# A table decides which picks' V rows VectorE sums: from a flat quarter to 0 to 12 of each 16

## The chip, the cores and the metric

The kernel runs as one program on one core of a Trainium2 chip. The metric is the device time of one execution in microseconds; the median of several runs counts.

## The reference

One inference step of a two-layer decoder in fp32, for 512 prompt tokens and 8 sample tokens, width 1024. Each layer is a recurrent mixer (layer 0: gated DeltaNet and Mamba-2 side by side; layer 1: gated linear attention) and then a PEER block, which picks for each token 8 x 16 = 128 of 16384 single-neuron experts:

```python
v1, i1 = lax.top_k(s1, PEER_TOPK)
v2, i2 = lax.top_k(s2, PEER_TOPK)
cand = (v1[..., :, None] + v2[..., None, :]).reshape(...)
top_s, top_j = lax.top_k(cand, PEER_TOPK)
expert = jnp.take_along_axis(cand_idx, top_j, axis=-1)
gate = jax.nn.softmax(top_s, axis=-1)
pre = jnp.einsum('thkd,td->thk', u_tab[expert], tb)
act = jax.nn.gelu(pre) * gate
return jnp.einsum('thk,thkd->td', act, v_tab[expert])
```

The tables are too large for on-chip memory, so each pick is a gather of one U row and one V row (8 KB together) for each of 128 tokens: 1 MB.

## The kernel before

**Units and picks.** Tokens are cut into tiles of 128 prompt tokens and one of 8 sample tokens. A unit is one layer and one tile; the ten units are the outer loop (layer 0: tiles 0, 1, sample, 2, 3, then layer 1 the same), and units 2 and 7 are those of the sample. A unit of prompt tokens has 128 picks, one of the sample 8, in all 1040 picks, numbered by g. In this text a stretch is 16 picks of one unit, from the dot product of its first pick to that of the next stretch.

**One pick.** GpSimd (POOL) issues the gather into one of 7 slots of `ring` (L456). VectorE (DVE) waits for it, multiplies the U half with the tokens and sums: the dot product (L1817). ScalarE (ACT) makes gelu of it (`act_v`), multiplies by the gate (`gated`) and, for most picks, scales the identity matrix by it into one of 4 slots of `diag`. TensorE (PE) then multiplies `diag` with the V half of the slot, two products 128x512 that add up in PSUM banks 0 and 1 over the unit. That counts `v_done`, and the slot is free for the gather of pick g + 7.

**Picks aside.** For picks marked in the table `ASIDE` no `diag` is made and PE does nothing. Instead VectorE multiplies the V half by the weight and adds it to `otok` (`add_v`, L1778; the first of a unit only multiplies, L1776), after the dot product of pick g + 2, and counts `side_done`, for which POOL waits then. At the end of a unit VectorE adds PSUM to `otok` (`join_out`, L1785), and PE transposes it back. `SUMMED` and `TURNED` count the picks of either kind up to g, and every engine takes its waits from them.

```python
ASIDE = [t != S and u < 8 and k % 4 == 2 for u, (_, t) in enumerate(UNITS) for k in range(COUNT[u])]
```

**The other work.** The mixers, the output and query projections and the rankings of later tiles (top 16, twice) are generators that yield a slot, the number of a pick; each engine runs all their work of slot g behind its work for pick g (`front.upto(g)`, `choose.upto(g)`), PE two picks ahead (`LEAD`). Weight products (`ps<-hT,wring`) take 6 matmuls of PE a slot, and SyncE loads their weights in blocks of 512 KB into 3 slots of `wring`. So the table of slots fixes which stretches stand beside products, convolutions, scans or rankings. Rankings run on VectorE (L1643 to L1678). Every engine works in order.

Of the kernel before, what the change touches and what calls it, by code (L numbers as in the profile page):

```python
# [36 lines left out]
S = 4  # L37
# [11 lines left out]
UNITS = [(L, t) for L in range(2) for t in (0, 1, S, 2, 3)]  # L49
COUNT = [NS_TOK if t == S else NPICK for _, t in UNITS]  # L50
FIRST = [sum(COUNT[:u]) for u in range(len(UNITS) + 1)]


ASIDE = [t != S and u < 8 and k % 4 == 2 for u, (_, t) in enumerate(UNITS) for k in range(COUNT[u])]
SUMMED = [sum(ASIDE[:g]) for g in range(len(ASIDE) + 1)]
TURNED = [g - n for g, n in enumerate(SUMMED)]
HAS_ASIDE = [any(ASIDE[FIRST[u]:FIRST[u + 1]]) for u in range(len(UNITS))]
HSLOT = (0, 1, 0, 1, 2)
# [51 lines left out]
def build_program(nc, io):  # L110
# [5 lines left out]
    with ExitStack() as ctx:  # L116
# [5 lines left out]
        def sem(name):  # L122
            if name not in sems:
                sems[name] = ctx.enter_context(nc.semaphore(name))
            return sems[name]
# [235 lines left out]
        def _(pool):  # L361
# [82 lines left out]
            for u, (L, t) in enumerate(UNITS):  # L444
# [4 lines left out]
                for k in range(COUNT[u]):  # L449
                    g = FIRST[u] + k  # L450
                    index = tail_pick[:, k:k + 1] if t == S else picked[:, HSLOT[t], k:k + 1]
                    if g >= RING and ASIDE[g - RING]:
                        pool.wait_ge(sem("side_done"), SUMMED[g - RING + 1])
# [15 lines left out]
        def _(pe):  # L469
# [396 lines left out]
            for u, (L, t) in enumerate(UNITS):  # L866
# [9 lines left out]
                for k in range(COUNT[u]):  # L876
                    g = FIRST[u] + k
                    if not ASIDE[g]:
                        pe.wait_ge(sem("weighed"), TURNED[g + 1])
# [22 lines left out]
        def _(act):  # L902
            def f(out, in_, func, **k):
                return act.activation(out, in_, func, **k)  # L904
# [213 lines left out]
            for u, (L, t) in enumerate(UNITS):  # L1118
                for k in range(COUNT[u]):
# [6 lines left out]
                    f(gated[:, s:s + 1], act_v[:, s:s + 1], ACT.Copy, scale=gate).then_inc(sem("gated"), 1)  # L1126
                    if not ASIDE[g]:
                        act.wait_ge(sem("gated"), g + 1)
# [20 lines left out]
        def _(dve):  # L1149
# [619 lines left out]
            def add_v(g):  # L1769
                u = [v for v in range(len(UNITS)) if FIRST[v] <= g][-1]  # L1770
                weight = gated[:, g % SMALL:g % SMALL + 1]
                dve.wait_ge(sem("gated"), g + 1)
                if SUMMED[g] == SUMMED[FIRST[u]]:
                    if u:
                        dve.wait_ge(sem("out_mm"), u)
                    last = tsc(otok[:, :], ring[:, g % RING, D:2 * D], weight, None, MUL)  # L1776
                else:
                    last = stt(otok[:, :], ring[:, g % RING, D:2 * D], weight, otok[:, :], MUL, ADD)  # L1778
                last.then_inc(sem("side_done"), 1)

            def join_out(u):
                dve.wait_ge(sem("v_done"), TURNED[FIRST[u + 1]])
                dve.wait_ge(sem("side_done"), SUMMED[FIRST[u + 1]])
                x = otok.rearrange("p (b i) -> p b i", b=2)
                tt(x, x, ps[:, 0:2, :], ADD).then_inc(sem("otok_ready"), 1)  # L1785

            def add_out(u):
                dve.wait_ge(sem("out_mm"), u + 1)
                t = UNITS[u][1]
                x = xT[:, :, TILE_AT[t]:TILE_AT[t] + ROWS[t]]  # L1790
                if t == S:
                    y = ps[:, 0, 0:KD * NS_TOK].rearrange("p (c b) -> p c b", c=KD)
                else:
                    y = ps[:, 0:2, :].rearrange("p b (c i) -> p (b c) i", c=4)
                tt(x, x, y, ADD).then_inc(sem("added"), 1)
# [4 lines left out]
            for u, (L, t) in enumerate(UNITS):  # L1800
                if t != S:
                    dve.wait_ge(sem("htok_ready"), u + 1)
                if t == S:
                    add_v(FIRST[u] - 2)
                    join_out(u - 1)
                for k in range(COUNT[u]):
                    g = FIRST[u] + k
                    if t == S:
                        dve.wait_ge(sem("spread"), L * NS_TOK + k + 1)
                        h = ps[:, 4 + 2 * (k % 2):6 + 2 * (k % 2), :]  # L1810
                    else:
                        h = htok[:, HSLOT[t], :]
                    dve.wait_ge(sem(f"uv_loaded{g % RING}"), 16 * (g // RING + 1))
                    x = ring[:, g % RING, 0:D]
                    if t == S:
                        x = x.rearrange("p (b i) -> p b i", b=2)
                    stt(x, x, 1.0, h, MUL, MUL, accum_out=pre[:, g % SMALL:g % SMALL + 1]).then_inc(sem("dotted"), 1)  # L1817
                    if g >= 2 and ASIDE[g - 2] and not (t == S and k == 0):
                        add_v(g - 2)
                    if k == 0 and u and t != S and HAS_ASIDE[u - 1]:  # L1820
                        join_out(u - 1)
                    if k == 1 and u:
                        add_out(u - 1)
                    front.upto(g)
                    choose.upto(g)
# [116 lines left out]
```

## Time and profile before

| | |
|---|---|
| median of 3 runs | 3783.91 us (3767.95 to 3787.49) |
| profiled execution | 3767.21 us, its span 3765.4 us |
| PE / DVE / ACT / POOL busy | 78% / 65% / 32% / 33% |
| HBM traffic over the span | 325 GB/s |
| dot products L1817 | 1024 + 16, 1226 ns each for 128x1024 |
| adds L1778 | 186, 1286 ns each |
| gathers L456 | 1024 in the largest group, 1151 ns of issue each |

Busy shares are averages over stretches with different limits, so the reading goes by stretch. In tables by stretch a line has the stretch in us from the span's start, its length, and then busy us with the number of instructions for PE, PEld (weight load of PE, which overlaps PE), DVE, ACT and POOL; then the granted clock of PE as a share of full speed, the mean busy share of the 16 DMA engines, and GB/s moved.

### The profile page before, as it was taken

Reading aid. Unit: us, or ns where it says so; the run is one execution under the profiler, and the core shown is the slowest. Engines: PE = TensorE matmul, PEld = TensorE weight load, DVE = VectorE, ACT = ScalarE, POOL = GpSimd, SP = SyncE. Lnnn points to the kernel's source line nnn. Section 1 sums busy time; section 2 is a strip of 40 time slices with the busy share of each in tenths; the row PEclk is TensorE's granted clock in tenths of the full one; section 3 lists DMA queues with packets and bytes.
Section 4 is the critical chain, followed back from the end, with each engine's and each line's share of the span. In section 5 each row is a group of like instructions: output and inputs, shape, how many; then the busy total and the mean of one; then the engine's idle time right before and its main releaser. Section 6 shows DMA issues by size and latency. Waiting matters only on the chain.

```text
span 3765.4 us, 31261 instructions
## 1 busy us (share of the span) xinstructions
PE 2942.9 (78%) x9704; PEld 1695.3 (45%) x9704; DVE 2448.8 (65%) x5019; ACT 1190.9 (32%) x3448; POOL 1245.4 (33%) x1094
## 2 busy tenths in 40 slices
PE   7667478788789769998976679887896678778776
PEld 6556345455556325655632237454563223222222
DVE  4333579688665778676569787557656958645444
ACT  1211133533233323343333332422333324334333
POOL 0000022355333423343345433334334434434332
PEclk9788788899789979989989889888899889999999
DMA  4102187899899979988999999879899879999996
GB/s 153 55 1 90 56 315 264 321 374 364 323 360 392 385 274 342 360 334 344 395 417 412 373 396 364 329 291 404 338 391 406 338 287 412 395 420 418 417 420 287
DMA packets 183658, 1225.39 MB, mean 325 GB/s; under 512 B 21185, under 2 KB 21585, under 8 KB 48194
## 3 DMA queue, kind: packets, MB, share of 16 engines
q0 software_dynamic: 153088, 1115.26, 74.7%
q1 hardware_dynamic: 30402, 108.12, 7.7%
q8 instruction: 77, 1.26, 0.1%
q14 instruction: 91, 0.75, 0.1%
HBM read 1211.46 MB, written 11.84 MB: 325 GB/s over the span
## 4 chain that ended last, share of the span: by engine, by line
PE 42%; DVE 25%; DMA 20%; ACT 4%; issue 3%; DVEq 2%; POOL 2%; SPq 0%; ACTq 0%; POOLq 0%
PE ps L471 42%; DMA ring<-in_uv,picked 19%; DVE ring L1817 7%; DVE otok L1778 2%; POOL ring L456 2%; ACT scratch L904 2%; DVE scratch L1645 1%; DVE scratch L1647 1%; DVE scratch L1651 1%; DVEq L1641 1%; DVE scratch L1643 1%; DVE scratch L1676 1%; DVE scratch L1671 1%; DVE ids L1678 1%; ACT diag L904 1%
## 5 line engine op out<-in xcount | busy, mean ns | idle before, releaser
L471 PE MATMUL ps<-ring,diag 128*128 128x512 f32 x3392 | 1782.2, 658 | 493.8 <-ACT diag L904 485.5
L456 POOL DMA_INDIRECT ring<-in_uv,picked x1024 | 1178.7, 1151 | 2100.7 <-PE ps L471 1413.7
L1817 DVE SCALAR_TENSOR_TENSOR ring<-ring,htok 128x1024 f32<-128x1024 f32 x1024 | 1246.1, 1226 | 653.1 <-DMA ring<-in_uv,picked 639.6
L471 PEld LDWEIGHTS ps<-ring,diag 128*128 128x128 f32 x3392 | 645.3, 204 | 1379.7 <-ACT diag L904 826.1
L471 PE MATMUL ps<-hT,wring 128*128 128x256 f32 (+1 forms) x3200 | 744.2, 388 | 62.2 <-DVE hT L1187 28.2
L904 ACT ACTIVATE act_v<-pre 128x1 f32<-128x1 f32 x1040 | 209.6, 202 | 1697.0 <-DVE ring L1817 1687.6
L471 PEld LDWEIGHTS ps<-hT,wring 128*128 128x128 f32 x3200 | 618.0, 194 | 232.0 <-issue 97.2
L904 ACT ACTIVATE diag<-masks,gated 128x128 f32<-128x128 f32 x832 | 334.1, 402 | 44.6 <-PE ps L471 17.4
L904 ACT ACTIVATE gated<-act_v,gates 128x1 f32<-128x1 f32 x1024 | 301.6, 295 | 33.3
L471 PE MATMUL ps<-scratch 128*128 128x128 f32 (+4 forms) x1424 | 234.6, 313 | 73.5 <-ACT scratch L904 23.4
L471 PEld LDWEIGHTS ps<-scratch 128*128 128x128 f32 (+2 forms) x1424 | 203.4, 209 | 146.8 <-issue 56.7
L1778 DVE SCALAR_TENSOR_TENSOR otok<-ring,gated,otok 128x1024 f32<-128x1024 f32 x186 | 239.1, 1286 | 0.0
L904 ACT ACTIVATE scratch<-ps 128x512 f32<-128x512 f32 (+6 forms) x114 | 68.8, 604 | 285.2 <-PE ps L471 281.1
L904 ACT ACT_TABLE_LOAD x101 | 129.6, 1283 | 3.1 <-DVEq L1155 1.4
L904 ACT ACTIVATE keep<-ps 128x256 f32<-128x256 f32 (+2 forms) x106 | 40.7, 384 | 266.6 <-PE ps L471 262.6
L382 POOL TENSOR_TENSOR scratch<-scratch,masks 128x512 f32<-128x512 f32 x24 | 32.9, 1380 | 237.5 <-DVE scratch L1309 221.2
L1643 DVE MAX8 scratch<-scratch 128x8 f32<-128x128 f32 (+1 forms) x192 | 50.3, 324 | 75.0 <-ACT scratch L904 74.2
L1817 DVE DVE_READ_ACCUMULATOR ring<-ring,htok 128x1 f32 x1024 | 83.8, 82 | 0.0
L1549 DVE SCALAR_TENSOR_TENSOR state<-state,scratch,ps 128x256 f32<-128x256 f32 x64 | 26.5, 476 | 68.1 <-PE ps L471 68.1
L471 PE MATMUL ps<-masks,keep 128*128 128x128 f32 x288 | 42.7, 302 | 35.8 <-DVEq L1155 33.1
L904 ACT ACTIVATE keep<-xT 128x256 f32<-128x256 f32 (+3 forms) x88 | 34.3, 392 | 111.5 <-DVE xT L1205 96.8
L1205 DVE TENSOR_TENSOR xT<-ps,xT 128x256 f32<-128x256 f32 (+1 forms) x32 | 13.7, 428 | 85.9 <-PE ps L471 85.9
(243 smaller groups left out, 1625.3 us busy)
## 6 DMA issues: line engine op xcount, KB each, us to landing
wring<-in_weights SPq DMA_DIRECT2D x200, 512.0 KB
ring<-in_uv,picked POOLq DMA_INDIRECT x1024
scratch<-in_keys POOLq DMA_DIRECT2D x4, 1024.0 KB, 14.1
scratch<-in_s_gla POOLq DMA_DIRECT2D x4, 1024.0 KB, 12.1
out_o_gla<-scratch POOLq DMA_DIRECT2D x4, 1024.0 KB, 12.9
xT<-in_xT SPq DMA_DIRECT2D x1, 2080.0 KB
scratch<-in_s_dn POOLq DMA_DIRECT2D x1, 2048.0 KB, 11.8
scratch<-in_s_ssm POOLq DMA_DIRECT2D x1, 2048.0 KB, 16.8
```

The source lines that it names most:

```text
L456: pool.indirect_dma_start(out=ring[:, g % RING, :], out_offset=None, in_=io["uv"][L], in_offset=bass.IndirectOffsetOnAxis(ap=index, axis=0 ...
L471: return pe.matmul(out, lhsT, rhs, start=start, stop=stop)
L904: return act.activation(out, in_, func, **k)
L1641: dve.drain()
L1643: dve.max(vals[:, 0:8], src)
L1645: dve.max_index(idx[:, 0:8], vals[:, 0:8], src)
L1647: dve.match_replace(out=src, in_to_replace=vals[:, 0:8], in_values=src, imm_value=-3e38)
L1651: dve.max_index(idx[:, 8:16], vals[:, 8:16], src)
L1671: tt(eq[R].rearrange("p h (k a) -> p (h k) a", a=TOPK), posf[R].rearrange("p h (k a) -> p (h k) a", a=1).to_broadcast([rows, NPICK, TOPK]) ...
L1676: tt(e4, e4, of.to_broadcast([rows, PH, TOPK, TOPK]), MUL)
L1778: last = stt(otok[:, :], ring[:, g % RING, D:2 * D], weight, otok[:, :], MUL, ADD)
L1817: stt(x, x, 1.0, h, MUL, MUL, accum_out=pre[:, g % SMALL:g % SMALL + 1]).then_inc(sem("dotted"), 1)
```

## The change

The rule "every fourth pick, k % 4 == 2, in units up to 6" becomes a table with one digit for each 16 picks of a unit: digit 0 puts none on VectorE, 1 one pick in four, 2 two in four, 3 three in four (k % 4 = 1, 2, 3), never the first or last pick of a unit. A wait on `side_done` is added ahead of each add but the first of a unit. At the sample units the add and the join are made only where the table asks for them.

```diff
--- before.py
+++ after.py
@@ -51,7 +51,10 @@
 FIRST = [sum(COUNT[:u]) for u in range(len(UNITS) + 1)]
 
 
-ASIDE = [t != S and u < 8 and k % 4 == 2 for u, (_, t) in enumerate(UNITS) for k in range(COUNT[u])]
+SHARE = {0: "00211111", 1: "11123100", 3: "01311133", 4: "30000000", 5: "01321111", 6: "12320000"}
+WHICH = ((), (2,), (1, 3), (1, 2, 3), (0, 1, 2, 3))
+ASIDE = [u in SHARE and 0 < k < COUNT[u] - 1 and k % 4 in WHICH[int(SHARE[u][k // 16])]
+         for u in range(len(UNITS)) for k in range(COUNT[u])]
 SUMMED = [sum(ASIDE[:g]) for g in range(len(ASIDE) + 1)]
 TURNED = [g - n for g, n in enumerate(SUMMED)]
 HAS_ASIDE = [any(ASIDE[FIRST[u]:FIRST[u + 1]]) for u in range(len(UNITS))]
@@ -1775,6 +1778,7 @@
                         dve.wait_ge(sem("out_mm"), u)
                     last = tsc(otok[:, :], ring[:, g % RING, D:2 * D], weight, None, MUL)
                 else:
+                    dve.wait_ge(sem("side_done"), SUMMED[g])
                     last = stt(otok[:, :], ring[:, g % RING, D:2 * D], weight, otok[:, :], MUL, ADD)
                 last.then_inc(sem("side_done"), 1)
 
@@ -1801,8 +1805,10 @@
                 if t != S:
                     dve.wait_ge(sem("htok_ready"), u + 1)
                 if t == S:
-                    add_v(FIRST[u] - 2)
-                    join_out(u - 1)
+                    if ASIDE[FIRST[u] - 2]:
+                        add_v(FIRST[u] - 2)
+                    if HAS_ASIDE[u - 1]:
+                        join_out(u - 1)
                 for k in range(COUNT[u]):
                     g = FIRST[u] + k
                     if t == S:
```

By the table 199 picks stand aside instead of 192. In 12 stretches there are more than before: 8 instead of 4 in five of them, 12 instead of 4 in six, 11 instead of 4 in one (75 more together). In 17 stretches there are none instead of 4 (68 fewer). In the remaining ones there are 4 as before.

VectorE in unit 6 from pick 34 on, beside the query projection; `ring,pre<-ring,htok` is a dot product, `otok<-` an add. Before:

```order
L1817 SCALAR_TENSOR_TENSOR ring,pre<-ring,htok 128x1024 [waits uv_loaded3]
L1817 SCALAR_TENSOR_TENSOR ring,pre<-ring,htok 128x1024 [waits uv_loaded4]
L1817 SCALAR_TENSOR_TENSOR ring,pre<-ring,htok 128x1024 [waits uv_loaded5]
L1778 SCALAR_TENSOR_TENSOR otok<-ring,gated,otok 128x1024 [waits gated]
L1817 SCALAR_TENSOR_TENSOR ring,pre<-ring,htok 128x1024 [waits uv_loaded6]
L1817 SCALAR_TENSOR_TENSOR ring,pre<-ring,htok 128x1024 [waits uv_loaded0]
L1817 SCALAR_TENSOR_TENSOR ring,pre<-ring,htok 128x1024 [waits uv_loaded1]
L1817 SCALAR_TENSOR_TENSOR ring,pre<-ring,htok 128x1024 [waits uv_loaded2]
L1778 SCALAR_TENSOR_TENSOR otok<-ring,gated,otok 128x1024 [waits gated]
```

Now:

```order
L1823 SCALAR_TENSOR_TENSOR ring,pre<-ring,htok 128x1024 [waits uv_loaded3]
L1823 SCALAR_TENSOR_TENSOR ring,pre<-ring,htok 128x1024 [waits uv_loaded4]
L1782 SCALAR_TENSOR_TENSOR otok<-ring,gated,otok 128x1024 [waits side_done,gated]
L1823 SCALAR_TENSOR_TENSOR ring,pre<-ring,htok 128x1024 [waits uv_loaded5]
L1782 SCALAR_TENSOR_TENSOR otok<-ring,gated,otok 128x1024 [waits side_done,gated]
L1823 SCALAR_TENSOR_TENSOR ring,pre<-ring,htok 128x1024 [waits uv_loaded6]
L1782 SCALAR_TENSOR_TENSOR otok<-ring,gated,otok 128x1024 [waits side_done,gated]
L1823 SCALAR_TENSOR_TENSOR ring,pre<-ring,htok 128x1024 [waits uv_loaded0]
L1823 SCALAR_TENSOR_TENSOR ring,pre<-ring,htok 128x1024 [waits uv_loaded1]
L1782 SCALAR_TENSOR_TENSOR otok<-ring,gated,otok 128x1024 [waits side_done,gated]
```

Each group of four dot products has three adds instead of one, and each add waits for the one before it too.

PE at the same place, where `ps<-hT,wring` are weight products and `ps<-ring,diag` the V rows of a pick. Before:

```order
L471 MATMUL ps<-ring,diag 128x512 [waits weighed]
L471 MATMUL ps<-ring,diag 128x512
L471 MATMUL ps<-hT,wring 128x264 x2
L471 MATMUL ps<-hT,wring 128x264 [waits gemm_free,w_loaded2]
L471 MATMUL ps<-hT,wring 128x264 x3
L471 MATMUL ps<-ring,diag 128x512 [waits weighed]
L471 MATMUL ps<-ring,diag 128x512
L471 MATMUL ps<-hT,wring 128x264 x4
L471 MATMUL ps<-hT,wring 128x264 [waits gemm_free,w_loaded0]
L471 MATMUL ps<-hT,wring 128x264
L471 MATMUL ps<-ring,diag 128x512 [waits weighed]
L471 MATMUL ps<-ring,diag 128x512
```

Now:

```order
L474 MATMUL ps<-ring,diag 128x512 [waits weighed]
L474 MATMUL ps<-ring,diag 128x512
L474 MATMUL ps<-hT,wring 128x264 x4
L474 MATMUL ps<-hT,wring 128x264 [waits gemm_free,w_loaded0]
L474 MATMUL ps<-hT,wring 128x264 x7
L474 MATMUL ps<-hT,wring 128x264 [waits gemm_free,w_loaded1]
L474 MATMUL ps<-hT,wring 128x264 x7
L474 MATMUL ps<-hT,wring 128x264 [waits gemm_free,w_loaded2]
L474 MATMUL ps<-hT,wring 128x264 x3
L474 MATMUL ps<-ring,diag 128x512 [waits weighed]
L474 MATMUL ps<-ring,diag 128x512
```

Three of four pairs of V products are gone, and the weight products between two pairs that are left stand in one run.

VectorE in unit 4 from pick 64 on, in the ranking of a later tile. Before:

```order
L1817 SCALAR_TENSOR_TENSOR ring,pre<-ring,htok 128x1024 [waits uv_loaded1]
L1778 SCALAR_TENSOR_TENSOR otok<-ring,gated,otok 128x1024 [waits gated]
L1643 MAX scratch<-scratch 128x8 x3
L1817 SCALAR_TENSOR_TENSOR ring,pre<-ring,htok 128x1024 [waits uv_loaded2]
L1643 MAX scratch<-scratch 128x8 x3
L1817 SCALAR_TENSOR_TENSOR ring,pre<-ring,htok 128x1024 [waits uv_loaded3]
L1645 MAX_INDEX scratch<-scratch 128x8 x3
L1817 SCALAR_TENSOR_TENSOR ring,pre<-ring,htok 128x1024 [waits uv_loaded4]
L1645 MAX_INDEX scratch<-scratch 128x8 x3
L1817 SCALAR_TENSOR_TENSOR ring,pre<-ring,htok 128x1024 [waits uv_loaded5]
L1778 SCALAR_TENSOR_TENSOR otok<-ring,gated,otok 128x1024 [waits gated]
```

Now:

```order
L1823 SCALAR_TENSOR_TENSOR ring,pre<-ring,htok 128x1024 [waits uv_loaded1]
L1646 MAX scratch<-scratch 128x8 x3
L1823 SCALAR_TENSOR_TENSOR ring,pre<-ring,htok 128x1024 [waits uv_loaded2]
L1646 MAX scratch<-scratch 128x8 x3
L1823 SCALAR_TENSOR_TENSOR ring,pre<-ring,htok 128x1024 [waits uv_loaded3]
L1648 MAX_INDEX scratch<-scratch 128x8 x3
L1823 SCALAR_TENSOR_TENSOR ring,pre<-ring,htok 128x1024 [waits uv_loaded4]
L1648 MAX_INDEX scratch<-scratch 128x8 x3
L1823 SCALAR_TENSOR_TENSOR ring,pre<-ring,htok 128x1024 [waits uv_loaded5]
```

The adds between the steps of the ranking are gone; their V rows are PE's.

## Rows read from the trace of the kernel before

**Rows 1.** Busy us by engine, clock, DMA share, GB/s of one stretch.

```profile
3258.70:3418.40 159.70, 127.05 (x257) 43.43 (x257) 78.95 (x129) 57.50 (x192) 62.18 (x65) 1.00 1.01 420
```

**Rows 2.** Table by stretch: twelve stretches of 16 picks beside weight products.

```profile
636.90:691.20 54.30, 50.60 (x182) 35.98 (x183) 35.66 (x78) 22.41 (x59) 15.76 (x15) 0.94 0.85 318
1116.20:1167.80 51.60, 47.46 (x167) 30.94 (x166) 32.61 (x55) 18.65 (x55) 19.12 (x17) 1.00 0.97 379
1167.80:1226.90 59.10, 59.10 (x227) 42.69 (x226) 24.57 (x36) 15.40 (x52) 15.50 (x15) 1.00 0.99 396
1539.00:1595.40 56.40, 51.24 (x170) 30.75 (x170) 29.99 (x45) 21.07 (x58) 18.66 (x16) 0.95 0.95 370
1744.10:1800.30 56.20, 52.56 (x187) 35.39 (x186) 34.87 (x64) 19.15 (x55) 19.72 (x18) 0.98 0.99 388
1800.30:1853.70 53.40, 53.40 (x208) 39.12 (x207) 24.54 (x39) 16.97 (x57) 16.13 (x15) 1.00 1.01 415
1853.70:1906.90 53.20, 45.47 (x152) 28.23 (x151) 25.94 (x38) 14.31 (x50) 20.59 (x18) 0.97 0.95 379
2306.60:2366.00 59.40, 59.40 (x228) 42.96 (x227) 32.15 (x44) 16.82 (x56) 17.92 (x16) 1.00 0.96 369
2366.00:2419.40 53.40, 42.80 (x135) 21.23 (x135) 35.81 (x53) 27.61 (x63) 19.95 (x18) 0.87 0.92 349
2702.60:2752.90 50.30, 46.55 (x165) 30.99 (x164) 33.37 (x57) 18.58 (x55) 18.39 (x17) 1.00 0.98 381
2752.90:2810.10 57.20, 57.20 (x218) 41.10 (x217) 24.53 (x36) 15.05 (x52) 15.73 (x15) 1.00 1.00 397
2810.10:2857.80 47.70, 37.71 (x105) 19.60 (x104) 24.52 (x36) 14.49 (x51) 22.02 (x19) 0.96 0.95 375
```

**Rows 3.** Waits in 2752.9 to 2810.1: who waited for whom, total, times, longest.

```profile
POOL ring L456 <- PE ps L471: 40.4, 11, 4.9
DVE ring L1817 <- DMA ring<-in_uv,picked: 31.8, 16, 5.4
```

**Rows 4.** Timeline of one product stretch: start, duration, engine, line, operation, tiles.

```profile
2764.10 1.88 PE L471 MATMUL ps<-ring,diag 128*128 128x512 f32 x4
...
2765.82 2.83 PE L471 MATMUL ps<-hT,wring 128*128 128x264 f32 x12
```

**Rows 5.** Table by stretch: five stretches of 16 picks beside rankings.

```profile
1274.10:1325.70 51.60, 36.12 (x102) 16.25 (x100) 45.64 (x170) 16.35 (x49) 22.72 (x19) 0.93 0.94 380
1325.70:1389.60 63.90, 34.45 (x62) 12.82 (x62) 56.16 (x116) 15.65 (x47) 18.82 (x18) 0.77 0.63 243
2029.40:2080.90 51.50, 29.81 (x48) 10.73 (x48) 50.37 (x109) 15.66 (x47) 23.39 (x16) 0.84 0.93 375
2944.80:2999.90 55.10, 30.59 (x50) 10.84 (x49) 53.96 (x196) 12.78 (x44) 22.52 (x16) 0.81 0.91 358
2999.90:3058.20 58.30, 34.04 (x64) 13.38 (x63) 43.11 (x59) 15.65 (x47) 22.02 (x18) 0.73 0.71 282
```

**Rows 6.** Chain of waits from 2029 to 2081: start, length, what.

```profile
2039.77 1.13 DVE ring L1817 x2
2040.90 1.20 DVE otok L1778
2042.09 0.80 DVE scratch L1645 x3
```

**Rows 7.** Chain of waits at the end of unit 1.

```profile
1374.04 10.56 PE ps L471 x20
```

**Rows 8.** Table by stretch: three other stretches whose adds go to TensorE.

```profile
543.50:636.90 93.40, 79.26 (x275) 54.04 (x273) 87.68 (x241) 29.97 (x68) 19.89 (x17) 0.93 0.78 286
1421.00:1467.40 46.40, 40.13 (x154) 25.80 (x154) 42.21 (x139) 21.90 (x60) 16.40 (x14) 0.93 0.88 336
2199.70:2248.80 49.10, 40.17 (x124) 22.55 (x123) 46.02 (x138) 20.99 (x57) 18.28 (x16) 0.83 0.97 388
```

**Rows 9.** Chain of waits after unit 6: one gather from issue to landing.

```profile
3037.67 11.47 DMA ring<-in_uv,picked
```

## Prediction

> **What bounds the kernel now.** I read the tables by stretch first, since the kernel's two kinds of limit lie in different stretches, and then the waits and the chain inside one stretch of each kind. The floor comes from a long stretch with nothing beside the picks: 159.7 us for 64 picks, 2.50 us each, at 420 GB/s and a DMA share of 1.01 [rows 1]. There PE has all V rows, is busy for 127.05 us (1.99 us a pick) and is not the limit. A prompt pick can't be cheaper than 2.50 us, so a stretch of 16 can't fall under 39.9 us.
>
> Beside weight products a stretch takes 47.7 to 59.4 us [rows 2]. In four of the twelve PE is busy without a gap at full clock, and in the last but one VectorE is busy for only 24.53 of 57.20 us. Its waits tell the rest: POOL waits 40.4 us for PE to free slots, and VectorE 31.8 us for gathers that were issued late for that reason [rows 3]. But the same rows have a second limit close behind: most of them move 369 to 415 GB/s, since the weights come on top of the gathers. Beside rankings the picture is the other one: VectorE is busy for 50.37 of 51.50 and 53.96 of 55.10 us [rows 5], and the chain goes dot product, add, ranking step without a gap [rows 6].
>
> **Beside products: 75 picks leave PE.** A pair of V products starts at 2764.10 and the next weight product at 2765.82, so a pick costs PE 1.72 us at full clock [rows 4]. Four picks fewer save it 6.9 us, eight 13.8, seven 12.0. Were PE the only limit, that would be 75 x 1.72 = 129 us. The bytes of a stretch don't shrink, though. A stretch can't be shorter than its length x its GB/s / 420, the rate of rows 1; the third of the list can go from 59.1 to 55.7 us, the sixth, at 415 GB/s, only from 53.4 to 52.8 [rows 2]. Taking for each of the twelve the smaller of what PE saves and what the bytes leave, in the order of the rows: 6.9, 5.0, 3.4, 6.7, 4.3, 0.6, 5.2, 7.2, 6.9, 4.7, 3.1, 5.1, together 59 us. This is a ceiling: it needs gathers and weights to keep the DMA engines full throughout, and in the first, the ninth and the tenth stretch PE has gaps already, in which something else is waited for. The bounds are 0 (the DMA share stands at 0.95 to 1.00 in most of these stretches, which one may read as full) and 59. The nearest row to a full stretch with weights, 415 GB/s, is at the upper end; I take two thirds, **40 us**.
>
> VectorE must take the 75 adds at 1.20 us each in the chain [rows 6]. Eight more in a stretch are 9.6 us: 24.57 becomes 34.2 of 55.7, and the fullest stretches with eight more come to 34.87 + 9.6 = 44.5 of 51.9 and 32.15 + 9.6 = 41.8 of 52.2 [rows 2]. So the cover is the time in which it waits for gathers, and it is left with 7 us at the least. If that cover were gone the adds would cost up to 90 us. ScalarE loses one scaling of the identity for each such pick, which nothing waits for there. The new wait for the add before is met when it is reached, since a dot product of 1.2 us always stands between two adds; without the wait an add starts at 2040.90, where the dot product ends (2039.77 + 1.13) [rows 6]. I cost it at nothing. It could cost only where VectorE is the limit, and in those stretches there is no add left to wait.
>
> **Beside rankings: 20 picks leave VectorE.** Five stretches lose four adds each, 20 x 1.20 = 24.0 us off the chain [rows 5, 6]. PE takes the products; it is busy for 30 to 36 us of 51 to 64 there and has room, though at a clock of 0.73 to 0.93. Where it doesn't is the end of units 1 and 6: a run of products of five picks (20 records) takes 10.56 us after the last dot products and `join_out` waits for it [rows 7], 2.11 us a pick where the stretch's mean granted clock is 0.77 [rows 5]. There one pick more joins the run in each unit, the late one whose add is gone. 24.0 - 2 x 2.1 = **20 us**. Bounds: 0, if PE's in-order queue passes the picks' cost on, and 24, if the two runs at the ends cost nothing; the byte floor allows it, 46.0 us at 375 GB/s for the third.
>
> **The other stretches that lose their adds.** In the second stretch of unit 0 VectorE is busy for 87.68 of 93.40 us and PE for 79.26 [rows 8]: PE comes to 79.26 + 4 x 1.72 = 86.1, VectorE to 82.9, so the 4.8 us can be had. In the first of unit 3 PE would rise from 40.13 to 47.0 us, over the 46.40 that the stretch lasts: 0. In the first of unit 5 PE comes to 47.1 at the most and the stretch from 49.10 to there: 2.0. Together **7 us**. Six stretches in unit 4 and one in unit 6 run at or near the floor, where 16 V rows on PE fit [rows 1]: 0. Two more, the first of unit 0 and one late in unit 6, I leave at 0; they could give 4.8 each, or lose as much as PE's price, 6.9 each.
>
> **Sum.** 40 + 20 + 7 = 67 us. The profiled execution took 3767.2 us (its span 3765.4), so it would be 3700. The median of the runs shown is 3783.9, 16.7 above the profiled one, and their lowest agrees with it; the kernel scatters by 0.5% and I put half of that on top: **3708 us**. Half a percent (19 us) is also what I take as the least that a measurement can tell from no change.
>
> **Rivals.**
>
> *The transfers are full already.* A DMA share of 0.99 at 396 GB/s may mean that weights beside gathers don't run at 420. Then the twelve stretches stay and only 20 + 7 = 27 us come: 3740 for the profiled execution, 3748 with the same addition. For it: shares of 0.95 to 1.01 in ten of the twelve. Against it: one stretch with weights moves 415 GB/s [rows 2], and the waits name PE, not a full queue [rows 3]. The Trainium skill ("DMA: Bandwidth & Descriptors", Specifications) gives a limit of about 358 GB/s of HBM bandwidth per core; by it no product stretch could gain. Here the trace disagrees: 420 GB/s over 159.7 us [rows 1].
>
> *PE alone is the limit.* All 129 us come through, with the 27: 3611 + 8 = 3619. The byte floor would have to be wrong by more than 10%: the third stretch would have to run at 396 x 59.1 / 45.3 = 517 GB/s, above everything in these rows. It could hold only in part.
>
> *Slots are held too long, the kernel is slower.* An add frees its slot only after the dot product two picks later: two periods, 1.23 us of dot product (78.95 / 64) and 1.20 of add; issue takes 15.73 / 15 = 1.05 [rows 1, 2]. With flight F of a gather, seven slots turn in 7p = F + 2p + 3.5. One gather from issue to landing took 11.47 us [rows 9], which makes p = 3.0 us, 48 a stretch, under the byte floor of 52 to 56. Weights in the queue could stretch F. The seven stretches with twelve (or eleven) adds now last 56.4 us on average, 3.53 a pick. With F at 20 us p is 4.7, the stretch 75 us, and 7 x 18.8 = 132 us are lost against the 27 gained: 3872. It decides from F = 15.4 us, where p = 3.77 and 7 x 16 x 0.24 = 27. Against it: the picks already aside have this lag and POOL issues in order, yet it is PE that POOL waits for, 40.4 us in eleven waits [rows 3].
>
> *Nothing moves.* PE's price for the 68 picks that come back, at 1.72 to 2.11 us each (117 to 143 us), eats what the rest gives, if the stretches taken as slack aren't: within 19 us of before, 3765 to 3803. PE's busy time in rows 5 speaks against it.
>
> **Chances.** The forecast 0.66, full transfers 0.16, PE alone 0.04, slots held too long 0.06, nothing moves 0.08. Faster by over 0.5%: 0.66 + 0.16 + 0.04, and a little of the rest, 0.87. Within 0.5%: 0.08. Slower: 0.05. The range: below, ceilings of 59 + 24 + 7 + 10 = 100 us off 3767 give 3667, and the half-way through PE alone is left out; above, full transfers at 3748 and a few us for the two stretches that I left at 0. So 3660 to 3755. It holds the forecast and full transfers, 0.82.
>
> **What would show it.** In the new profile PE should no longer be busy throughout the seven densest product stretches, these should last 48 to 55 us at 390 to 420 GB/s, and VectorE should be busy there for 34 to 45 us. The five ranking stretches should be 4 to 5 us shorter each, the last two of units 1 and 6 less. POOL's waits should pass from PE to the adds. The forecast is wrong if product stretches keep their length at the GB/s of before (full transfers), if they fall below their byte floor (PE alone), or if VectorE waits longer for gathers at less than 370 GB/s (slots).

## The result

In the first series of runs the changed kernel takes 3745.0 us, median of 4 runs (3709.8 to 3747.9), against 3778.7 for the kernel before: ratio 0.9884, 95% interval 0.9842 to 0.9925. In a second series the same pair gave 0.9832 (0.9796 to 0.9868), 3732.6 against 3790.6 us. So the change makes the kernel 1.2 to 1.7% faster; 3708 us and 2.0% were forecast. The profiled execution took 3744.4 us, its span is 3742.6 us, 22.8 shorter than before. The time alone would speak for the first rival, full transfers, which gave 3748 us; what tells it from the forecast are the stretches below.

### The profile page after: what moved, and what is told of

The parts are those of the page before. It is cut to its first block, busy times and chain, and to the rows that moved or that the text cites. A ratio compares the mean times of both kernels' runs of the same rounds, so it can differ in the third digit from the quotient of the medians.

```text
span 3742.6 us, 31392 instructions
## 1 busy us (share of the span) xinstructions
PE 2952.1 (79%) x9676; PEld 1687.8 (45%) x9676; DVE 2459.2 (66%) x5026; ACT 1190.7 (32%) x3441; POOL 1215.5 (32%) x1094
## 4 chain that ended last, share of the span: by engine, by line
PE 38%; DMA 27%; DVE 22%; ACT 4%; issue 4%; DVEq 2%; POOL 1%; SPq 0%; ACTq 0%; POOLq 0%
PE ps L474 38%; DMA ring<-in_uv,picked 24%; DVE ring L1823 6%; DMA wring<-in_weights 2%; ACT scratch L907 2%; DVE otok L1782 1%; DVE scratch L1648 1%; POOL ring L459 1%; DVE scratch L1679 1%; DVE scratch L1674 1%; ACT diag L907 1%; DVE scratch L1650 1%; DVE scratch L1654 1%; DVE scratch L1646 1%; DVE ids L1681 1%
## 5 line engine op out<-in xcount | busy, mean ns | idle before, releaser
L474 PE MATMUL ps<-ring,diag 128*128 128x512 f32 (+1 forms) x3364 | 1757.9, 654 | 439.8 <-ACT diag L907 431.0
L459 POOL DMA_INDIRECT ring<-in_uv,picked x1024 | 1150.0, 1123 | 2098.7 <-PE ps L474 1566.7
L1823 DVE SCALAR_TENSOR_TENSOR ring<-ring,htok 128x1024 f32<-128x1024 f32 x1024 | 1247.5, 1226 | 624.3 <-DMA ring<-in_uv,picked 617.3
L474 PEld LDWEIGHTS ps<-ring,diag 128*128 128x128 f32 (+1 forms) x3364 | 626.0, 201 | 1341.1 <-ACT diag L907 798.5
L1782 DVE SCALAR_TENSOR_TENSOR otok<-ring,gated,otok 128x1024 f32<-128x1024 f32 x193 | 248.4, 1287 | 0.0
L1823 DVE SCALAR_TENSOR_TENSOR ring<-ring,ps 128x1024 f32<-128x1024 f32 x16 | 19.5, 1221 | 73.0 <-PE ps L474 73.0
L474 PEld LDWEIGHTS ps<-masks,keep 128*128 128x128 f32 x288 | 44.1, 228 | 51.7 <-issue 51.7
## 6 DMA issues: line engine op xcount, KB each, us to landing
ring<-in_uv,picked POOLq DMA_INDIRECT x1024, 10.7
```

The lines of the kernel that those rows point to most:

```text
L459: pool.indirect_dma_start(out=ring[:, g % RING, :], out_offset=None, in_=io["uv"][L], in_offset=bass.IndirectOffsetOnAxis(ap=index, axis=0 ...
L474: return pe.matmul(out, lhsT, rhs, start=start, stop=stop)
```

## The profile after

The twelve stretches beside products in the table by stretch of the changed kernel, as in [rows 2], with their sum:

```profile
640.90:691.70 50.80, 46.98 (x172) 34.21 (x173) 38.64 (x82) 22.06 (x58) 14.49 (x13) 0.93 0.82 318
1106.30:1155.70 49.40, 43.32 (x147) 28.94 (x146) 37.34 (x60) 16.80 (x51) 17.30 (x16) 0.93 0.98 381
1155.70:1216.70 61.00, 56.15 (x230) 43.12 (x228) 32.99 (x44) 13.23 (x48) 17.01 (x18) 1.00 1.01 418
1538.70:1593.60 54.90, 39.89 (x140) 25.30 (x138) 38.35 (x52) 18.73 (x50) 17.66 (x16) 0.85 0.99 392
1753.10:1807.70 54.60, 41.85 (x157) 30.66 (x156) 43.05 (x71) 16.62 (x50) 19.09 (x17) 0.92 1.01 413
1807.70:1862.20 54.50, 50.07 (x205) 38.56 (x204) 33.86 (x45) 13.22 (x48) 20.79 (x17) 0.99 1.00 404
1862.20:1909.60 47.40, 29.20 (x92) 18.14 (x90) 34.83 (x46) 11.15 (x41) 20.79 (x16) 0.80 1.01 412
2305.50:2362.10 56.60, 55.57 (x225) 40.64 (x223) 40.47 (x52) 14.39 (x52) 23.10 (x17) 1.00 0.99 398
2362.10:2411.30 49.20, 33.95 (x95) 18.91 (x95) 41.67 (x60) 26.72 (x59) 20.59 (x15) 0.72 0.90 352
2682.90:2731.20 48.30, 40.24 (x142) 27.15 (x141) 37.98 (x62) 16.61 (x49) 17.29 (x15) 0.93 0.97 378
2731.20:2790.50 59.30, 55.24 (x219) 41.91 (x218) 32.92 (x44) 13.34 (x48) 19.98 (x18) 0.97 1.01 416
2790.50:2831.10 40.60, 28.02 (x66) 13.19 (x65) 30.47 (x41) 12.24 (x43) 22.18 (x16) 0.81 1.01 419
sum 626.60, PE 520.48 PEld 360.72 DVE 442.56 ACT 195.12 POOL 230.28; mean PE 43.37 PEld 30.06 DVE 36.88 ACT 16.26 POOL 19.19
```

The same sum for the kernel before:

```profile
sum 652.20, PE 603.50 PEld 398.99 DVE 358.56 ACT 220.50 POOL 219.48; mean PE 50.29 PEld 33.25 DVE 29.88 ACT 18.38 POOL 18.29
```

The stretches are 25.6 us shorter together, PE is busy for 83 us less and VectorE for 84 us more. PE now has gaps, but where it was busy throughout before, the gain is small or none: the third went from 59.1 to 61.0 us, the sixth from 53.4 to 54.5, the last but one from 57.2 to 59.3. They now move 404 to 418 GB/s at a DMA share of 1.00 or more, close to the rate of [rows 1]. The most is gained in the seventh, 53.2 to 47.4, and the last, 47.7 to 40.6 us. Both are now shorter than the floor that their old bytes gave (48.0 and 42.6 us), because they move fewer bytes than before (19.5 for 20.2 MB and 17.0 for 17.9 MB, length times GB/s).

POOL's waits in the third of these stretches (1155.7 to 1216.7), who waited for whom, us in total, times, longest:

```profile
POOL ring L459 <- DVE otok L1782: 27.8, 10, 4.1
POOL ring L459 <- PE ps L474: 18.3, 6, 4.9
```

and in the eleventh (2731.2 to 2790.5) those of POOL and PE:

```profile
POOL ring L459 <- PE ps L474: 25.5, 6, 5.9
POOL ring L459 <- DVE otok L1782: 14.8, 7, 4.5
...
PEld ps L474 <- DMA wring<-in_weights: 6.2, 5, 2.5
...
PE ps L474 <- DMA wring<-in_weights: 4.1, 4, 2.1
```

In the third POOL waits longer for the adds than for PE. In the eleventh PE is still what POOL waits for longest, 25.5 us where it was 40.4 [rows 3], and the adds came in with 14.8. But PE now has gaps there, and it waits 4.1 us for weights, at a DMA share of 1.01: PE is held up in part by the transfers. The ranking stretches, to be set beside [rows 5]:

```profile
1261.80:1309.60 47.80, 40.67 (x118) 18.11 (x116) 42.10 (x167) 17.97 (x53) 20.19 (x21) 0.99 0.95 384
1309.60:1373.80 64.20, 39.31 (x77) 15.36 (x78) 50.34 (x112) 17.27 (x51) 19.26 (x17) 0.85 0.76 288
2032.50:2080.50 48.00, 35.92 (x64) 11.85 (x64) 45.54 (x105) 17.26 (x51) 21.54 (x17) 0.87 1.01 417
2917.70:2967.60 49.90, 34.54 (x69) 12.03 (x67) 49.11 (x191) 14.38 (x48) 16.80 (x17) 0.97 0.98 393
2967.60:3022.80 55.20, 36.85 (x79) 14.31 (x78) 37.22 (x53) 17.26 (x51) 18.08 (x17) 0.86 0.77 295
sum 265.10, PE 187.29 PEld 71.65 DVE 224.31 ACT 84.14 POOL 95.87; mean PE 37.46 PEld 14.33 DVE 44.86 ACT 16.83 POOL 19.17
```

They are 15.3 us shorter in sum (280.4 before), though the second isn't shorter at all. The third is now at 417 GB/s and a share of 1.01, that is at the transfers' limit, so it gave 3.5 us and not 4.8. The three stretches of [rows 8] went from 188.9 us to:

```profile
sum 181.30, PE 164.13 PEld 104.65 DVE 164.10 ACT 78.38 POOL 55.03; mean PE 54.71 PEld 34.88 DVE 54.70 ACT 26.13 POOL 18.34
```

What no step of the forecast has in it are the stretches of the two sample units. Of the kernel before:

```profile
1389.60:1421.00 31.40, 28.95 (x56) 6.76 (x55) 12.06 (x21) 6.90 (x26) 5.62 (x6) 0.86 0.84 301
3058.20:3089.30 31.10, 28.65 (x55) 6.73 (x55) 10.87 (x18) 5.59 (x21) 5.63 (x6) 0.85 0.75 264
```

and of the changed one:

```profile
1373.80:1419.80 46.00, 43.54 (x56) 9.36 (x55) 12.01 (x20) 6.87 (x26) 5.62 (x6) 0.58 0.48 169
3022.80:3064.80 42.00, 39.55 (x55) 8.79 (x55) 10.87 (x16) 5.58 (x21) 5.62 (x6) 0.62 0.54 190
```

The instructions are the same, but PE ran at a granted clock of 0.58 and 0.62 instead of 0.86 and 0.85, and both together take 25.5 us more. In the chain of waits of the changed kernel from 1340 to 1420 (start, length, what):

```profile
1354.39 14.19 PE ps L474 x28
...
1379.61 38.51 PE ps L474 x48
```

28 records of V products, seven picks, stand ahead of the join, where five stood in [rows 7]. Then 48 records of the sample unit's products take 38.51 us. In the same chain of the kernel before:

```profile
1395.43 23.85 PE ps L471 x48
```

The parts add up: -25.6 beside products, -15.3 beside rankings, -7.6 in the three others, +25.5 in the sample units, and 0.2 in all the rest: 22.8 us. This rest isn't still, it cancels: the first pick starts 10.9 us later (486.1 for 475.2 us; the other traces have 478.7 to 489.4, so the trace of before is the early one), and the remaining stretches give 10.7 us, of which 6.9 are the first stretch of unit 1, which went from 73.6 to 66.7 us here and took 73.9 in the next trace of the changed kernel.

## Experiments

All tables were applied to the changed kernel; where a diff shows a new `SHARE` alone, it replaces that of the changed kernel. Sums "of the twelve" and "of the five" are those of the product and ranking stretches between the dot products of the same picks, from each kernel's own profiled execution. Ratios are to the kernel before in the same series.

### The changed kernel again

No edit.

> The changed kernel as it is, for comparison on the same chip. Measured so far: 3745 us median, ratio 0.988. Every theory expects 0.984 to 0.993. In its trace I look at the two sample stretches (picks 256 to 263 and 776 to 783), which took 46.0 and 42.0 us instead of 31.4 and 31.1. If their length is an effect of the change they are over 40 us again; if it was chance of the clock they fall back to 31 to 35.

Measured: 3732.6 us, ratio 0.9832 (0.9796 to 0.9868), a little under the lower end of what was expected. The twelve took 625.8 us and the five 264.2 us, within 1 us of the first trace, while the profiled execution was 15 us longer. Stretch sums repeat better than the time of a run, so the further experiments are read by them. How well shows over all traces: with the changed kernel's digits beside products the twelve took 626.6, 625.8, 630.0 and 624.3 us, with a quarter in them 652.2, 655.5, 659.2 and 658.5, means of 626.7 and 656.4. The sample stretches were 42.5 and 45.5 us, at clocks of 0.63 and 0.57: over 40 again.

### Products alone and removals alone

```diff
-SHARE = {0: "00211111", 1: "11123100", 3: "01311133", 4: "30000000", 5: "01321111", 6: "12320000"}
+SHARE = {0: "11211111", 1: "11123111", 3: "11311133", 4: "31111111", 5: "11321111", 6: "12321111"}
```

> Only the twelve stretches beside products keep their larger digits, every 0 becomes 1. By the byte floor (my forecast, with the 26 us that the new trace shows in these stretches) the time is 3752 to 3760 us against 3779, ratio 0.993 to 0.996. If the transfers were full before (first rival) it is 1.000. If PE alone were the limit it would be 129 us less, ratio 0.966. The sample stretches stay at 31 us, since the last adds of units 1 and 6 are back.

Measured: ratio 0.9892 (0.9843 to 0.9941), lower than the 0.993 to 0.996 expected, which the upper end of the interval just takes in. The last line of the table for the twelve and for the five:

```profile
sum 630.00, PE 518.38 PEld 358.62 DVE 443.88 ACT 195.65 POOL 230.33; mean PE 43.20 PEld 29.88 DVE 36.99 ACT 16.30 POOL 19.19
```

```profile
sum 282.80, PE 165.92 PEld 64.02 DVE 249.47 ACT 76.09 POOL 107.08; mean PE 33.18 PEld 12.80 DVE 49.89 ACT 15.22 POOL 21.42
```

```diff
-SHARE = {0: "00211111", 1: "11123100", 3: "01311133", 4: "30000000", 5: "01321111", 6: "12320000"}
+SHARE = {0: "00111111", 1: "11111100", 3: "01111111", 4: "10000000", 5: "01111111", 6: "11110000"}
```

> Only the seventeen stretches with 0 adds keep them, every 2 and 3 becomes 1. Theory A: the removals give 15 us beside rankings and 8 us in three other stretches, and lose 25 us in the two sample stretches, because the last V rows now stand on PE at the lower clock: ratio 0.998 to 1.003. Theory B: the slow sample stretches are chance: 23 us less, ratio 0.994.

Measured: ratio 0.9940 (0.9909 to 0.9971). Again the last lines for the twelve and the five, and then its two sample stretches:

```profile
sum 655.50, PE 604.89 PEld 398.81 DVE 356.65 ACT 220.51 POOL 218.07; mean PE 50.41 PEld 33.23 DVE 29.72 ACT 18.38 POOL 18.17
```

```profile
sum 264.30, PE 183.15 PEld 70.57 DVE 224.70 ACT 84.11 POOL 94.97; mean PE 36.63 PEld 14.11 DVE 44.94 ACT 16.82 POOL 18.99
```

```profile
1396.70:1443.00 46.30, 43.56 (x57) 9.42 (x55) 12.07 (x21) 7.24 (x28) 5.63 (x7) 0.58 0.49 177
3072.40:3102.10 29.70, 27.24 (x55) 6.58 (x54) 10.82 (x16) 5.59 (x21) 5.62 (x6) 0.89 0.79 286
```

Each half acts where it is made and nowhere else. With products alone the twelve take 630.0 us and the five 282.8 (652.2 and 280.4 before). With removals alone the five take 264.3 and the twelve 655.5. The effects of the two on the time, 1.1% and 0.6%, make up the 1.7% of both in that series. Both halves are faster than before by themselves. The time of the removals alone is what theory B gives, but its first sample stretch is slow as in theory A and its second is not, so the sample unit had to be looked at by itself.

### The ends of units 1 and 6

```diff
-SHARE = {... 1: "11123100", ... 6: "12320000"}
+SHARE = {... 1: "11123101", ... 6: "12320001"}
```

> The changed table with the last digit of units 1 and 6 at 1 instead of 0, eight picks. Theory A (late V rows on PE slow the sample unit): the sample stretches go back to about 31 us, the last ranking stretches get up to 5 us longer each, together 15 us less than the changed kernel, ratio to before 0.984. Theory B (chance of the clock): 5 to 10 us more than the changed kernel, 0.990.

Measured: ratio 0.9853 (0.9817 to 0.9890), not to be told from the changed kernel. The first sample stretch was 31.9 us at clock 0.84, the second 41.9 us at 0.62. The five took 267.2 us.

```diff
+SHARE = {0: "11111111", 1: "11111110", 3: "11111111", 4: "11111111", 5: "11111111", 6: "11111110"}
```

> A quarter everywhere as in the kernel before, but none in the last 16 picks of units 1 and 6. If the late V rows on PE make the sample stretches slow, both are over 40 us and the time is 15 to 20 us over before, less 8 us for the shorter last ranking stretches. If it needs the other zeros ahead of them (a clock that has risen earlier and falls there), they stay at 31 us.

Measured: ratio 1.0018 (0.9977 to 1.0058). Its sample stretches:

```profile
1402.40:1434.00 31.60, 29.14 (x56) 6.78 (x55) 11.98 (x20) 6.82 (x26) 5.62 (x6) 0.85 0.73 271
3077.20:3118.60 41.40, 38.94 (x55) 8.59 (x54) 10.91 (x18) 5.59 (x21) 5.62 (x6) 0.63 0.58 212
```

Theories that make the slow sample unit a sure effect of the last digit, or of the other zeros, are both refuted: the first stretch of each kernel is quick. Over all traces the tally is this. In four kernels with a quarter in the last two stretches of units 1 and 6 (before, products alone, the wait alone, half weights before) the two sample stretches took 62.5, 62.3, 70.2 and 62.8 us together. In seven traces with zeros in all of these (the changed one twice, removals alone, half at most, earlier add, half weights, half and earlier add) they took 88.0, 88.0, 76.0, 65.1, 79.2, 91.3 and 62.3. The mean is 64.5 in the first and 78.6 in the second group, 14 us apart. In each slow case the clock is at 0.53 to 0.68 on average, in each quick one at 0.79 to 0.89. The two kernels of this section, with a zero in only one of the last two digits of both units, stand between the groups with 73.8 and 73.0 us. Counted one by one, 1 of 8 sample stretches is slow (over 38 us) in the first group, 8 of 14 in the second and 2 of 4 in these two. So the zeros seem to make the lower clock more frequent there, but so few traces don't show it; what decides it in one execution stays open.

### How many adds are worth having

```diff
+SHARE = {0: "00211111", 1: "11122100", 3: "01211122", 4: "20000000", 5: "01221111", 6: "12220000"}
```

> Every 3 in the table becomes a 2: 8 adds instead of 12 in seven stretches, 27 picks back to PE. By the byte floor PE's saving above what the bytes leave was worth nothing: the twelve product stretches stay at 626 us within 6, the time within 0.3% of the changed kernel. If PE's time still counts there, 27 x 1.72 = 46 us come back, most of them: 650 us and more for the twelve.

Measured: 3722.3 us, ratio 0.9817 (0.9749 to 0.9884). The twelve:

```profile
sum 628.00, PE 557.79 PEld 378.37 DVE 412.25 ACT 205.43 POOL 224.57; mean PE 46.48 PEld 31.53 DVE 34.35 ACT 17.12 POOL 18.71
```

27 picks went back to PE, whose busy time rises from 520 to 558 us, and the twelve last 628.0 us instead of 626.6. The adds beyond 8 of 16 bought nothing that can be told from the spread.

### When a slot is freed

```diff
-                    if g >= 2 and ASIDE[g - 2] and not (t == S and k == 0):
-                        add_v(g - 2)
+                    if g >= 1 and ASIDE[g - 1]:
+                        add_v(g - 1)
```

> Changed kernel with each add behind the dot product of the next pick instead of the next but one, so that a slot is free about one pick (3.5 us) earlier. By the byte floor nothing changes (product stretches 626 us within 6). If slots were held too long (third rival) the seven stretches with 11 or 12 adds get shorter, by up to 5 us each.

The run's name says later, but the add is made earlier, as the text has it. The part of the edit that isn't shown takes out the separate add at the start of a sample unit, which this loop now makes before. Measured: 3721.7 us, ratio 0.9811 (0.9730 to 0.9891). The twelve:

```profile
sum 617.50, PE 512.55 PEld 357.52 DVE 439.65 ACT 192.94 POOL 234.75; mean PE 42.71 PEld 29.79 DVE 36.64 ACT 16.08 POOL 19.56
```

617.5 against 626.6 and 625.8 us in the two traces of the changed kernel: 8 to 9 us. The seven stretches with 11 or 12 adds have 8.9 of it (388.3 to 379.4 us in sum), though not each of them: the eighth went from 56.6 to 53.9, the fifth from 54.6 to 52.2 and the sixth from 54.5 to 52.0, but the eleventh from 59.3 to 60.4. It is one trace, 7 us under the lowest of the four above. It comes from another chip than at least three of those four; a table with a quarter beside products took 659.2 us on that chip, so the chip isn't what made it quick.

Both edits together, the table with at most half and the earlier add:

> A candidate for a better version: at most 8 adds of 16 picks, each add one pick earlier. The earlier add took the product stretches from 626 to 618 us with 12 adds; with at most 8 fewer slots are held long, so 615 to 622 us are expected, and a ratio of 0.978 to 0.984. It beats the changed kernel only if slots freed late still cost something at 8 adds.

Measured: 3724.5 us, ratio 0.9830 (0.9793 to 0.9868); the twelve took 621.7 us, against 628.0 with the later add, the same sign again, 6 us. So slots held too long, the third rival's mechanism, may cost some 6 to 9 us; both comparisons are of single traces and not far outside the spread of such sums, so it isn't shown. The candidate doesn't gain on either of its parts: none of the three variants can be told from the changed kernel by its time.

### The wait alone

```diff
+SHARE = {0: "11111111", 1: "11111111", 3: "11111111", 4: "11111111", 5: "11111111", 6: "11111111"}
```

> The picks aside of the kernel before (a quarter throughout) with the new wait of each add for the add before. I costed the wait at nothing: ratio 0.998 to 1.002. If it costs 0.09 us for each of 186 adds, and that all on the chain, it is 17 us, 1.0045.

Measured: ratio 1.0015 (0.9984 to 1.0045), no difference that can be told; the upper end of the interval still allows the 0.09 us per add. The ranking stretch at picks 64 to 79 of unit 4, where VectorE is the limit and four adds stand in the chain, took 51.5 us with the wait as without it. That leaves the wait no price there.

### Half of the weight bytes

```diff
-                    sp.dma_start(wring[:, b % WSLOTS, :, :].rearrange("p k c -> p (k c)"), io["weights"][BASE[name] + j])\
-                        .then_inc(sem(f"w_loaded{b % WSLOTS}"), 16)
+                    dst, src = wring[:, b % WSLOTS, :, :].rearrange("p k c -> p (k c)"), io["weights"][BASE[name] + j]
+                    if b >= WSLOTS:
+                        dst, src = dst[:, 0:D // 2], src[:, 0:D // 2]
+                    sp.dma_start(dst, src).then_inc(sem(f"w_loaded{b % WSLOTS}"), 16)
```

> The changed kernel with only the first half of each weight block loaded (256 of 512 KB, from the fourth block on; the products use what stands in the other half, so the mixers compute something else). Fewer bytes, the same instructions. If the bytes bound the twelve product stretches after the change, they fall from 626 us to about 570 (weights are 5 to 28% of their bytes, half of it goes, and DVE and PE bound the rest). If PE or the adds bound them they stay over 610.

> The same with the kernel before. If PE bounds its product stretches, as I read the waits, they stay near 652 us, over 635. If the transfers were full already (first rival) they fall as much as in the changed kernel.

The second is the same edit to the kernel before. Each has one execution; the twelve of the changed kernel:

```profile
sum 592.80, PE 510.02 PEld 358.59 DVE 441.02 ACT 192.73 POOL 233.42; mean PE 42.50 PEld 29.88 DVE 36.75 ACT 16.06 POOL 19.45
```

and of the kernel before:

```profile
sum 650.90, PE 603.92 PEld 399.68 DVE 357.75 ACT 217.95 POOL 214.80; mean PE 50.33 PEld 33.31 DVE 29.81 ACT 18.16 POOL 17.90
```

The same loss of bytes shortens the changed kernel's product stretches by 33.8 us (626.6 to 592.8) and those of before by 1.3 (652.2 to 650.9), or 5.5 from the mean of 656.4, hardly more than traces differ. The third and the eleventh stretch, which the change had not shortened, show it best. With half the weights before:

```profile
1183.20:1243.70 60.50, 60.50 (x229) 43.17 (x229) 24.56 (x37) 15.78 (x56) 15.97 (x15) 1.00 0.92 340
...
2759.80:2820.10 60.30, 60.30 (x228) 43.14 (x227) 24.51 (x36) 14.50 (x52) 16.62 (x16) 1.00 0.92 340
```

and after:

```profile
1169.80:1220.20 50.40, 50.40 (x212) 39.79 (x211) 32.91 (x44) 12.61 (x46) 19.07 (x16) 1.00 1.02 412
...
2710.20:2763.20 53.00, 52.56 (x216) 40.54 (x216) 32.98 (x44) 12.65 (x48) 19.13 (x17) 1.00 1.01 402
```

Before, PE is busy throughout and 340 GB/s is enough; fewer bytes don't help. After, the stretch falls by 10.6 and 6.3 us until PE is busy throughout, or nearly so, again. So PE bounded these two stretches before the change and the transfers bound them after it. With half of the weight bytes gone in both kernels, the adds would have been worth 650.9 - 592.8 = 58 us instead of 26. The 592.8 lie between the about 570 that was expected of full transfers and the 610 that would have spoken against them: not all of the time that bytes should cost came back.

A second way to the weights' lateness wasn't separated from the first. PE could wait because only three weight blocks can be under way, each of which lands some 8 us after its issue (median 8.1 us around the third stretch). A fourth slot would tell, but it doesn't fit: one tile then needs 45600 bytes of a partition where 41696 are left. Halved blocks don't tell, since they may also land sooner. In the third and the eleventh stretch a share of 1.01 at 416 to 418 GB/s speaks for the rate; in the others this stays open.

## Why the prediction was right, and where its sizes were off

**The limits of the densest stretches were read rightly.** "POOL waits for PE to free slots", with "a second limit close behind", is what half the weight bytes show from both sides. The first rival (transfers full already) is refuted: 25.6 us came beside products, and fewer bytes alone brought next to nothing before. That the measured 3745 us lie beside its 3748 is chance: beside products came 14 us fewer than forecast but 26 more than by the rival, and 25.5 us went in the sample units, which neither has in it. The 3745 lie in the upper part of the range, which had been kept for this rival. The limit of about 358 GB/s per core in the Trainium skill ("DMA: Bandwidth & Descriptors", Specifications) doesn't bind this run on one core: the third stretch moves 418 GB/s. The same page of the Trainium skill (Bandwidth) says of that figure that it is roughly what each core gets when both cores of an HBM domain stream, a case that no run here has. The second (PE alone is the limit, 129 us) is refuted too: the twelve gave 25.6 us, and 27 of the picks could go back to PE for 1.4 us.

**Beside products, 40 us: mis-sized, 25.6 measured, 30 by the means of four traces each.** The floor of a stretch was worked out from the bytes that it moved before. That step failed for single stretches, and three of the seven densest lasted 56.6 to 61.0 us, over the 48 to 55 that were named as the sign: an engine that is no longer late works off its backlog and asks for its next weights sooner. The third stretch moved 396 GB/s in 59.1 us, 23.4 MB, and now 418 GB/s in 61.0 us, 25.5 MB. It was forecast at 55.7 us with the old bytes. At the full rate 25.5 MB take 60.7 us, which is what it took. The stretch behind it has fewer weights to fetch, but the two together last 106.1 us as before (106.2). So two thirds of the ceiling of 59 us was still too much; it was 43 to 50%.

Bytes that move forward leave other stretches, though, and over the twelve their sum is the same: 245.5 MB before and 245.9 after by length times GB/s, 585 us at 420 GB/s, where 626.6 were measured. So the shift alone doesn't explain what is missing. The six stretches that now run at 404 GB/s or more (third, fifth, sixth, seventh and the last two) gave 9.4 us of the 21.7 that their floors left. The six others, at 318 to 398 GB/s, gave 16.2 of 37.4, which is the larger part of the 33 us missing. There the other assumption of the ceiling failed, that PE's saving comes through until the bytes are full: POOL still waits most for PE in four of them (20.9 to 32.7 us each) and for the adds in the other two (17.3 and 19.4 us). The transfers have a part there too: the DMA share is 0.97 to 0.99 in four of the six, and halved weight blocks take the six from 309.2 to 298.2 us. The prediction named three stretches in which PE had gaps before; its rows show eight [rows 2]. How the 21 us divide between these causes stays open.

**Beside rankings, 20 us: 15.3 measured, 19 by the means** (282.4 over four traces with a quarter, 263.7 over seven with zeros). Where nothing else stepped in the price of 1.20 us an add, 4.8 a stretch, was about right: 5.2 us in the fourth of the five, 3.8 in the first. The third is stopped by the byte floor: by its old bytes that was 46.0 us, and it is 48.0 us at 417 GB/s, the same mis-step as above. In the second nothing was gained (63.9 to 64.2 us). I had allowed one more pick in the last run, 2.1 of 4.8 us; two more joined it, and the run took 14.19 us for 10.56, 3.6 more.

**The three others, 7 us: 7.6 measured.** The first of unit 3 gave 2.0 us instead of 0: PE is busy for 41.25 us there and not for the 47.0 that I had added up. A part is that its clock rose from 0.93 to 1.00: adding 1.72 us a pick to a busy time taken at a lower clock overstates it, here by about 3 us (40.13 x 0.07). The rest is work that left the stretch, since it holds 163 records where 154 + 16 were counted. The first of the three gave 3.6 us of its 4.8, the last 2.0 as forecast.

**Sample units, 0: +25.5 us in this trace, 14 on the mean of seven.** No step had them in view. The prediction took the late V rows as 2.1 us a unit and looked for no effect behind the join. With the measured means the sum is 30 + 19 + 8 - 14 = 43 us, 1.1%. That is inside the first series' interval (0.75 to 1.58%) and a little under the second's (1.32 to 2.04%).

**The new wait, 0: bounded.** 1.0015 (0.9984 to 1.0045) and an unchanged 51.5 us where it would be on the chain.

**Slots held too long.** As a rival that turns the sign it was wrong; p = 3.0 us of slot time was below the byte floor as worked out. As a small cost, 6 to 9 us, it may be there, which the experiments leave open; the flight had been taken from one gather. POOL's waits passed to the adds only in part, against what was named as a sign.

**Addition for the median.** 8 us were put on top because three runs lay above the profiled one. The runs of one kernel spread over 0.5 to 1.5% of its time, so the profiled execution is one draw: in the first series it lay 0.6 us under the median of the changed kernel, in the second 26.9 above it. The stretches that differ most between two traces of the same kernel are scans with another granted clock: the first of unit 1 took 66.7 us at 0.82 in one and 73.9 at 0.72 in the other.

## What to carry to other kernels

When work leaves an engine that is late, don't take the next limit from the bytes that a stretch moved while it was late: that engine will pull its own loads forward, and the transfers must be summed over the whole backlog. And a stretch that isn't full of bytes isn't free either: look at who is waited for in each before the saving is counted in full. Move only as much as brings the engine to the next limit; here half of the picks did what three quarters did. A time that comes out near a rival's says little where several terms are off; compare the stretches. To tell two limits that lie close together, take away half of one resource's load in both kernels and compare the same stretches, since sums of stretches repeat within 7 us here where the time of a run doesn't within 30.

## What the runs showed of the hardware

TensorE's granted clock alternates between the full level (2.4 GHz) and half of it (1.2 GHz) through the whole kernel, and which stretch gets the lower one isn't the same in two executions of one program. The sample unit, 56 records of large matmuls with short waits, takes 31 us at a mean of 0.86 and 46 us at 0.58; ahead of it PE worked off a run of five or seven picks after waiting for VectorE. A run of 20 records took 10.56 us and one of 28 took 14.19 us, 0.53 and 0.51 us a record, so the length of that run itself isn't the surprise; the products behind it are. The sum of the two sample stretches lay between 62.3 and 91.3 us in seven traces with zeros at the ends, a spread as large as most effects that were tested here. In the quick cases the lower level was granted for 7 to 17 us from about the start of the sample unit on, in the slow ones for 27 to 48 us; why, no run told. The 30 us just ahead don't decide it: in the changed kernel with half of the weight bytes and in the one with at most half of the adds, each made earlier, they are alike (PE busy for 21.85 and 21.84 us in 45 records each, clock 0.74 and 0.75), and the first sample stretch then took 49.4 us at 0.53 in one and 31.4 us at 0.86 in the other.
